# Inverse's levels 1 to 4 as four tiles of 64 rows by 32 columns, level 5 as 32x32 tiles

## The reference

```python
def gated_delta_rule(q, k, v, g, beta):
    ...
    kb = kc * bc[..., None]
    m = jnp.where(strict, jnp.einsum('nbhid,nbhjd->nbhij', kb, kc) * decay, 0.0)
    eye = jnp.eye(CHUNK, dtype=f32)
    t_inv = lax.linalg.triangular_solve(eye + m, jnp.broadcast_to(eye, m.shape), left_side=True, lower=True)
    u = t_inv @ (vc * bc[..., None])
    w = t_inv @ (kb * jnp.exp(gcum)[..., None])
    ...
```

## Time and profile before

| | |
|---|---|
| median of 3 runs | 2671.15 us (2670.33 to 2674.09) |
| the profiled execution | 2671.84 us, span 2670.0 us |
| PE busy | 2629.2 us, 98% |
| weight loads (PEld) | 2381.3 us, 89% |
| DVE busy | 1625.9 us, 61% |
| ACT busy | 494.6 us, 19% |
| POOL busy | 160.5 us, 6% |
| mean granted clock | 0.997 |

### The profile page before, as it was taken

The page is one execution under the profiler, slowest core; times in us unless marked ns, Lnnn a source line. Parts: engine busy times, 40 slices in busy tenths (PEclk is TensorE's granted clock), DMA queues, the critical chain, the costliest instruction groups (busy, mean ns, idle before and its releaser), DMA issues.

```text
span 2670.0 us, 42927 instructions
## 1 busy us (share of the span) xinstructions
PE 2629.2 (98%) x17876; PEld 2381.3 (89%) x17876; DVE 1625.9 (61%) x3377; ACT 494.6 (19%) x867; POOL 160.5 (6%) x138
## 2 busy tenths in 40 slices
PE   9999999999999999999999999999999999999998
PEld 8899888788999999888878999988889998888998
DVE  4587665755677778665664666444357752324776
ACT  1011343321000100243431100013210011211000
POOL 0000000000430330000000240000000000000000
PEclk9999999999999999999999999999999999999999
DMA  9887431526446556531345444442344444333442
GB/s 378 307 331 276 158 112 64 197 95 237 174 159 244 205 207 221 213 142 66 135 151 187 159 172 162 157 174 95 126 142 157 158 159 167 125 142 111 159 157 95
DMA packets 74451, 458.96 MB, mean 172 GB/s; under 512 B 8308, under 2 KB 9216, under 8 KB 28176
## 3 DMA queue, kind: packets, MB, share of 16 engines
q1 hardware_dynamic: 73120, 449.34, 46.0%
q0 software_dynamic: 1136, 6.86, 0.7%
HBM read 455.08 MB, written 1.09 MB: 171 GB/s over the span
## 4 chain that ended last, share of the span: by engine, by line
PE 90%; DVE 5%; DMA 1%; DVEq 1%; ACT 1%; issue 1%; ACTq 0%
PE psum L544 19%; PE psum L718 14%; PE psum L776 14%; PE psum L625 9%; PE psum L942 8%; PE psum L824 4%; PE psum L1003 2%; PE psum L601 2%; PE psum L731 2%; PE psum L962 2%; PE psum L647 2%; PE psum L889 2%; PE psum L660 1%; DMA aring<-astream 1%; PE psum L836 1%; DVE aring L1872 1%
## 5 line engine op out<-in xcount | busy, mean ns | idle before, releaser
L544 PE MATMUL psum<-h,ring 128*128 128x256 f32 x1536 | 334.8, 379 | 1.4 <-DVE arena L1846 0.8
L544 PEld LDWEIGHTS psum<-h,ring 128*128 128x128 f32 x1536 | 291.4, 190 | 42.2 <-DVE arena L1846 1.1
L776 PE MATMUL psum<-arena 128*128 128x128 f32 x2112 | 249.7, 275 | 0.4 <-DVE arena L1746 0.4
L776 PEld LDWEIGHTS psum<-arena 128*128 128x128 f32 x2112 | 242.6, 192 | 0.6 <-DVE arena L1746 0.6
L625 PE MATMUL psum<-aring,ring 128*128 128x256 f32 x1088 | 237.3, 379 | 1.7 <-issue 1.7
L942 PE MATMUL psum<-h,ring 128*128 128x256 f32 x1024 | 235.0, 382 | 0.0
L625 PEld LDWEIGHTS psum<-aring,ring 128*128 128x128 f32 x1088 | 205.9, 190 | 29.8 <-issue 2.4
L942 PEld LDWEIGHTS psum<-h,ring 128*128 128x128 f32 x1024 | 190.3, 190 | 28.9 <-issue 3.6
L776 PE MATMUL psum<-arena,ring 128*128 128x128 f32 x1584 | 191.6, 275 | 0.0
L776 PEld LDWEIGHTS psum<-arena,ring 128*128 128x128 f32 x1584 | 184.3, 192 | 0.2
L718 PE MATMUL psum<-arena 128*128 128x128 f32 x1440 | 170.6, 275 | 0.0
(11 more groups left out here) (463 smaller groups left out, 3863.5 us busy)
## 6 DMA issues: line engine op xcount, KB each, us to landing
ring<-wstream SPq DMA_DIRECT2D x349, 1024.0 KB, 4.8
aring<-astream SPq DMA_DIRECT2D x128, 512.0 KB, 4.8
arena<-astream SPq DMA_DIRECT2D x16, 512.0 KB, 18.4
arena<-wstream SPq DMA_DIRECT2D x3, 1024.0 KB, 20.3
arena<-decays POOLq DMA_DIRECT2D x2, 1024.0 KB, 4.9
sq<-decays POOLq DMA_DIRECT2D x2, 1024.0 KB, 4.7
kst<-const SPq DMA_DIRECT2D x1, 1280.5 KB, 7.8
x<-xT SPq DMA_DIRECT2D x1, 1024.0 KB, 4.8
```

What stands on the lines that cost most here:

```text
L544: mm = pe.matmul(out, lhsT=tile_at(at[0] % RING, t), rhs=rhs(k), start=k == 0, stop=k == kt - 1)
L776: mm = pe.matmul(out, lhsT=w, rhs=v, start=m == 0 and name in ("M1", "M5", "M3", "M4"), stop=m == NF // 2 - 1, skip_group_check=True)
```

## The change

The levels 1 to 4 stay inside diagonal blocks of 32x32. They are now done in `quad_products`, with four tiles: tile b takes 64 rows (`BLOCKS[b // 2]`, the chunk) and 32 columns (`QUADS[b]`), and has 32 moving columns. The moving and copied blocks are kept compactly: TC (TI) and XC (X) have for each row the 32 columns of its own diagonal block. The masks are no longer multiplied into MT per level; NEAR is MT, negated, within the 32x32 blocks, and DVE multiplies the level's mask into X while it copies it out of PSUM, for both halves (ACT copied the low half before). TC is now copied by ACT alone. There is a second fill point in each level, `turn`, behind banks 2 and 4. Level 5 uses 32x32 tiles on MT itself, its sign is put in by the copies (scale -1.0), and the two halves of TQ hold the finished inverse of the low chunk. The 896 columns of level masks in the constants become 416 (`pairs`, `near`, four of 32 and `unit`).

```diff
-MIX_FILL = dict(keys=28, queries=16, decay0=41, ti0=4, level01=10, level02=10, level03=2, level04=2, level05=2,
+MIX_FILL = dict(keys=28, queries=16, decay0=41, ti0=1, level01=9, turn01=1, level02=9, turn02=1, level03=2, turn03=1,
+                level04=2, turn04=1, level05=2,
                 rb0=6, u00=3, state0=2, carry0=5, u10=2,
-                decay1=24, ti1=4, level11=2, level12=2, level13=2, level14=2, level15=2, rb1=6, u01=3, state1=2,
+                decay1=24, ti1=1, level11=2, turn11=1, level12=2, turn12=1, level13=2, turn13=1, level14=2,
+                turn14=1, level15=2, rb1=6, u01=3, state1=2,
...
+                def quad_products(bank, lhs, rhs, signals, start, stop):
                     for u in range(8):
-                        for r in blocks:
-                            rows = BLOCKS[r]
-                            mm = pe.matmul(psum[rows, bank + r, 64 * u:64 * u + 64], lhsT=lhs(rows, u), rhs=rhs(rows, u),
-                                           skip_group_check=True, **{n: f(u) for n, f in flags.items()})
-                            if u == 7:
-                                mm.then_inc(signals[r], 1)
+                        for b in range(4):
+                            mm = pe.matmul(psum[QUADS[b], bank + b // 2, 32 * u:32 * u + 32], lhsT=lhs(b, u),
+                                           rhs=rhs(b, u), start=start(u), stop=stop, skip_group_check=True)
+                            if u == 7 and b in signals:
+                                mm.then_inc(signals[b], 1)
...
-                for s in range(1, 6):
-                    pe.wait_ge(operands_of_act, cnt.next("operands_of_act"))
-                    pe.wait_ge(operands_of_dve, cnt.next("operands_of_dve", 2 if s == 1 else 1))
-                    square_products(0, own(EBS[s % 2]), own(TI), **alone)
-                    fill(f"level{g}{s}")
-                    pe.wait_ge(operands_of_act, cnt.next("operands_of_act", 1 if s == 1 else 3))
-                    pe.wait_ge(operands_of_dve, cnt.next("operands_of_dve"))
-                    square_products(2, own(TTI), own(XB), (0, 1) if s < 5 else (0,), **adds)
-                    square_products(4, own(XB), own(TTI), signals=(products_for_act, products_for_act if s < 5 else products_for_dve), **adds)
+                for s in range(1, 5):
+                    pe.wait_ge(operands_of_act, cnt.next("operands_of_act"))
+                    if s == 1:
+                        pe.wait_ge(operands_of_dve, cnt.next("operands_of_dve"))
+                    quad_products(0, own(NEAR), compact(TC), {3: products_for_dve}, lambda u: True, True)
+                    fill(f"level{g}{s}")
+                    if s > 1:
+                        pe.wait_ge(operands_of_act, cnt.next("operands_of_act"))
+                    pe.wait_ge(operands_of_dve, cnt.next("operands_of_dve", 1 if s == 1 else 2))
+                    quad_products(2, own(TTI), compact(XC), {3: products_for_act}, lambda u: False, False)
+                    quad_products(4, compact(XC), own(TTI), {1: products_for_act, 3: products_for_dve}, lambda u: False, False)
+                    fill(f"turn{g}{s}")
...
+                pe.wait_ge(operands_of_act, cnt.next("operands_of_act", 2))
+                pe.wait_ge(operands_of_dve, cnt.next("operands_of_dve", 2))
+                for u in range(8):
+                    out = slice(256 + 32 * u, 288 + 32 * u)
+                    for r in range(2):
+                        even, odd = QUADS[2 * r], QUADS[2 * r + 1]
+                        if r == 0:
+                            mm = pe.matmul(psum[odd, 2, out], lhsT=TTI[odd, u, odd], rhs=XC[odd, u], start=True, stop=True,
+                                           skip_group_check=True)
+                            if u == 7:
+                                mm.then_inc(products_for_act, 1)
+                        mm = pe.matmul(psum[even, 4 + r, out], lhsT=XC[odd, u], rhs=TTI[odd, u, odd], start=True,
+                                       stop=True, skip_group_check=True)
...
-                    for s in range(1, 6):
-                        take(XB[high, :, high], 1, high).then_inc(operands_of_dve, 1)
-                        last = TT(EBS[(s + 1) % 2], MT, lev(s + 1), ALU.mult)
+                    for s in range(1, 5):
+                        product()
+                        for r, rows in enumerate(BLOCKS):
+                            last = TT(XC[rows], quads_of(r, rows), all_units(level[s - 1][rows]), ALU.mult)
+                        last.then_inc(operands_of_dve, 1)
                         if g == 0 and s in (1, 2):
                             convolve(layer, 9 + s)
-                        if s < 5:
-                            take(TI[high, :, high], 3, high).then_inc(operands_of_dve, 1)
-                        else:
-                            last.then_inc(operands_of_dve, 1)
-                            take(TTI[high, :, high], 5, high).then_inc(operands_of_dve, 1)
+                        product()
+                        for b in (2, 3):
+                            last = V.tensor_copy(TTI[QUADS[b], :, QUADS[b]], quads_of(5, QUADS[b]))
+                        last.then_inc(operands_of_dve, 1)
```

More of the change, by code:

```diff
@@ L99 @@
            lq1=64, lk1=64, lq2=64, lk2=64)
-_CK = dict(ones=128, ident=128, cmask=512, bmask=512, upper=128, levels=7 * 128, rot=128, half=256,
+_CK = dict(ones=128, ident=128, cmask=512, bmask=512, upper=128, pairs=128, near=128, levels=4 * 32, unit=32, rot=128, half=256,
            freq=1)
@@ L195, in build @@
         ones, ident, upper, rot = K("ones"), K("ident"), K("upper"), K("rot")
[L196 removed]
+        level = [kst[:, CK["levels"][0] + 32 * s:CK["levels"][0] + 32 * (s + 1)] for s in range(4)]
         half = [kst[:, CK["half"][0] + P * s:CK["half"][0] + P * (s + 1)] for s in range(2)]
@@ L1025, in inverse @@
                 mm.then_inc(products_for_dve, 1)
[L1026 to L1040 removed]
+                quad_products(4, units, own(TTI), {}, lambda u: u == 0, False)
@@ L1442, in mixer, with take, own @@
                     low, high = BLOCKS
[L1444 removed]
+                    def take(*parts, scale=1.0):
                         act.wait_ge(products_for_act, cnt.next("products_for_act"))
[L1446 to L1456 removed]
+                        for dst, src in parts:
+                            last = E(dst, src, ACT.Identity, scale=scale)
+                        last.then_inc(operands_of_act, 1)
+                    def own(b):
+                        return TTI[QUADS[b], :, QUADS[b]], quads_of(4 + b // 2, QUADS[b])
+                    for s in range(5):
+                        if s == 4:
+                            take((TQ[QUADS[0], :, 0:32], quads_of(2, QUADS[0])), (TQ[QUADS[1], :, 32:64], quads_of(2, QUADS[1])),
+                                 (TC[QUADS[2]], quads_of(3, QUADS[2])))
+                        else:
+                            take(*[(TC[rows], quads_of(2 + r, rows)) for r, rows in enumerate(BLOCKS)])
+                        if s > 0:
+                            take(own(0), own(1))
                         if g == 0 and s in (2, 3):
                             silu(8 + s)
[L1459 removed]
+                        move(f"turn{g}{s}" if s else f"ti{g}")
+                        if s < 4:
+                            move(f"level{g}{s + 1}")
+                    take((XC[QUADS[1]], quads_of(0, QUADS[1])), scale=-1.0)
+                    move(f"level{g}5")
+                    take((TQ[QUADS[1], :, 0:32], quads_of(2, QUADS[1], 256)))
+                    take((TTI[QUADS[0], :, QUADS[1]], quads_of(4, QUADS[0], 256)))
+                    take((XB[high, :, low], blocks_of(3, high)), scale=-1.0)
                     act.wait_ge(products_for_act, cnt.next("products_for_act"))
@@ L2284, in delta_rule @@
                     D()
-                    TT(EBS[0], MT, lev(0), ALU.mult)
+                    TT(PAIRS, MT, all_units(K("pairs")), ALU.mult)
                     D()
-                    TT(TTI, I8, EBS[0], ALU.subtract).then_inc(operands_of_dve, 1)
-                    TT(EBS[1], MT, lev(1), ALU.mult)
+                    TT(TTI, I8, PAIRS, ALU.subtract).then_inc(operands_of_dve, 1)
+                    TT(NEAR, MT, all_units(K("near")), ALU.mult)
                     low, high = BLOCKS
-                    def take(dst, bank, rows):
-                        product()
-                        return V.tensor_copy(dst, blocks_of(bank, rows))
@@ L2309, in delta_rule @@
+                    V.tensor_copy(TTI[low, :, high], blocks_of(4, low))
                     dve.wait_ge(functions_for_dve, cnt.next("functions_for_dve"))
@@ L2861, in constants @@
     never, always = np.full((P, P), NEG), np.zeros((P, P))
-    levels = []
-    for s in range(7):
+    pairs = (i[:, None] // 2 == i[None, :] // 2) & (i[None, :] % 2 == 1) & (i[:, None] % 2 == 0)
+    near = np.where(i[:, None] // 32 == i[None, :] // 32, -1.0, 0.0)
+    levels, q = [], np.arange(32)
+    for s in range(1, 5):
```

(6 more changed lines are left out.)

58 lines of the change are left out of this document (32 added, 26 removed).

## The result

| | before | after |
|---|---|---|
| median | 2672.86 us (6 runs, 2670.33 to 2678.60) | 2683.40 us (6 runs, 2678.44 to 2692.72) |
| ratio, 95% interval | | 1.0041 (1.0027 to 1.0055) |
| the profiled execution, span | 2671.84, 2670.0 us | 2680.73, 2678.6 us |
| mean granted clock | 0.997 | 0.994 |

The account below looks back on a forecast made before the run. PE was taken as the bound, busy 2629.2 of 2670.0 us. Each inverse falls to 15.49 us, saving 6.34 or 7.18, twice each 27.0; 2671.84 - 27.0 = 2644.8, forecast 2644, range 2640 to 2668.

Parts of the forecast that it names:

- The rule on small products: Passage on the skill's 25 ns minimum between matmul starts; as an engine-wide floor 32.0 us per inverse, 39 us slower in all.
- the burst: Eight weight loads in four tiles with seven products between, after a wait, begin within 0.08 us: 11 ns a record.
- 256 rounds at 31 ns: Small products of one inverse; each round, every tile handles one record; 31 ns at 32 columns, 57 at 64.
- the rival with a slower supply: PE fed more slowly than four tiles eat, still faster: at 12 ns a record 12 us saved, 2659; 17%.
- Slower: Instruction supply above 15 ns a record costs more than tiles give; 2690 at 20 ns, 2726 at 29 ns; 14%.
- 7.55 us: What one inverse costs outside the small-product rounds: 15.49 - 256 x 0.031.
- the four stretches: The inverse of two head groups in two layers: 15.49 us each without fills, in place of 21.83 and 22.67.
- the prices of the groups: Sets of small products inside the inverse: 0.66 us for 32 matmuls, 1.15 for 64, including 0.16 in and out.
- the new wait ahead of the eight 64x64 products: After level 5, PE stands until ACT has copied bank 2's product: 0.54 us.
- XC and TC are hidden: Copies in the levels: XC's 1.00 us under fills of 1.06; TC's 0.9 under 1.1 of PE work.
- nothing moves outside the stretches: Claim that the rest of the kernel, outside the four inverse stretches, keeps its times.
- the round: Each tile handles one record: 57 ns at 64 moving columns, 31 taken at 32, near a straight line in columns.

Follow-up runs that it names:

- Experiment 5: Kernel before, with 384 matmuls of 64x32 tiles, then 384 of 64x64, added behind its last product, results unread; 2709.45 us in one run.
- experiment 2: Changed kernel with each of the 15 fill tiles inside head group 1's inverse issued twice; 2686.61 us, ratio to before 1.0053.
- experiment 8: Changed kernel with fill tiles dealt 22 and 22 evenly over the levels and weight slabs loaded outside the inverses; 2678.90 us, ratio 1.0017.
- Experiment 6: Changed kernel, but products for banks 0 and 2 take 64x64 weights with 32 moving columns, 16 matmuls instead of 32; 2663.78 us, ratio to before 0.9964.
- experiment 1: Kernel before, with a dummy 64x64 matmul behind each product of levels 1 to 5, 224 more per inverse; 2710.10 us, ratio 1.0138.
- experiment 7: Changed kernel with the weight slabs that fell into the dense levels requested one or two fill jobs later; 2679.06 us, ratio 1.0024.

## Why the prediction was wrong

**The step that failed** is the one under "The rule on small products": "that is 11 ns a record in a burst of 15 instructions", with the conclusion that the burst speaks against a supply at 25 ns. So the sum, 256 rounds at 31 ns, put the supply of instructions at nothing, and the rival with a slower supply was priced at 12 ns a record on the strength of the 0.9 us that a packet takes to move. What the runs showed in its place: packets of 256 instructions come 3.6 to 3.7 us apart on average and never closer than 3.25, however short their transfer, and that average is 28 to 29 ns a record. Fifteen instructions are far fewer than a packet holds, so they can all have been there before the burst began; such a burst shows how fast PE can start instructions, never how fast they arrive. Experiment 5 shows both in one row of work: 9 ns a record as long as the store lasts, 29 ns after. The prediction said that no row settles it for hundreds of records, and gave 17% to a supply of 12 ns that would still be faster, and 14% to the rival that came true, *Slower*, in which the same supply is decided at 15 ns a record.

**The rival's size was off too**, in its form. It took (records x supply) + 7.55 us and added the fills, as if the supply slept during other work. At 29 ns that gave 2726; measured 2683. Packets arrive during the fills as well, so a stretch costs at least the larger of its work and its supply, less what was in store at its start. For group 1 that is 28.4 us of supply (2077 instructions at 3.5 us for 256) against 22.0 of work, and 30.89 measured, with a slab in the way of one packet and a piece at half clock. It is a lower bound and no price: in experiment 2 the stretch of group 1 has 28.5 us of work and 29.2 of supply and takes 34.5 and 32.9, and the evenly filled stretches of experiment 8 have 28.8 us of supply and take 31.3 to 32.5. The Trainium skill's figure (TensorE: Matmul & The Clock Gate, Part 1: never below about 25 ns from start to start) is refuted here as a limit on the starts of the whole engine, since 64 records in four tiles take 0.69 us, 11 ns each; for a long row of small products the supply comes to much the same size, 29 ns, and the rule pointed the right way. Whoever had followed it would have had the sign.

**A term that no rival had** is the clock. The prediction took 1.00 throughout. Behind some of the holes came the 1.2 GHz level, and the same piece went from 5.01 to 9.03 us. Between them the two terms make most of the miss. The profiled execution is 35.6 us longer than forecast (27.0 + 8.6). PE stands 20.3 us in the four stretches where 2.6 were foreseen, which is 17.7. The clock is at the lower level in four pieces of 27.3 us in all (391.2 to 404.9, 445.8 to 449.2, 1230.9 to 1237.7, 1282.1 to 1285.5), PE being busy for 26.4 of them; that is 13.2 us more than at full clock. The other 4.7 are the groups' prices (2.4, next paragraph) and what wasn't split further.

**What was right**: the prices of the groups, 0.69 us for 0.66 and 1.24 for 1.15 (34 ns a round for 31); the new wait ahead of the eight 64x64 products, 0.45 for 0.54, on ACT and in each inverse; that XC and TC are hidden, since no wait for DVE stands inside a level; and that nothing moves outside the stretches but by the clock behind them (5.5 us there, 0.3 the other way in all the rest). With all products at these prices and no hole the stretches would have been some 0.6 us longer than predicted, and the kernel about 2646.

**Right for the wrong reason** is the round. It was worked out as a slope in moving columns (57 ns at 64, 31 at 32). Experiment 6 has 64x64 weights with 32 moving columns, and a set takes 1.05 us like one with 64 moving columns (1.07 in the earlier trace rows): (1.05 - 0.16) / 16 = 56 ns. Halving the moving columns alone gave nothing; it is with the smaller weight tiles, four in place of two, that the round fell to 34. Whether that is the load of the weights or the way two records share a tile was not tried apart.

**Left open**: why experiment 1 costs 38 us. How much of it is supply, how much the clock and how much the dummies' own time on the array was not separated. How many instructions are held in store is known only from below: 234 records with their loads, 468 instructions, ran without a stop. And how the 10.5 us divide among rate, slabs and clock is not settled exactly, since each hole brings the others; by experiment 7 the slabs' part is about 4 us, give or take as much. Why packets come no closer than 3.25 us is open too: the rows of experiment 5 divide the cycle into three parts of 0.9 to 1.5 us each (burst to next packet, the packet itself, packet to next burst), but nothing was varied that would say what sets them.

## What to carry to other kernels

Before you cut products into smaller ones, count instructions in a stretch, loads included (four for each f32 matmul), and set 3.5 us for each 256 of them against the stretch's work, level by level: where supply is larger, PE stands, and its clock may fall on top. A burst behind a wait says nothing on that rate; look for a row of several hundred records, or count the packets of the instruction queue. A product that does useless work on zeros with half the instructions can be the faster one.
